# Prompt delta rule: the turns of v and k stand at other places in TensorE's order

## The reference

```python
qkv, new_conv = causal_conv(jnp.concatenate([q_a, k_a, v_a], axis=-1), conv_buf, conv_w)
qkv = jax.nn.silu(qkv.astype(f32))
q, k, v = jnp.split(qkv, [GDN_QK_WIDTH, 2 * GDN_QK_WIDTH], axis=-1)
q, k = l2norm(q) * GDN_DK ** -0.5, l2norm(k)
...
A = jnp.where(strict, jnp.einsum('nbhid,nbhjd->nbhij', kb, k) * decay, 0.0)
L = A + jnp.eye(C, dtype=A.dtype)
sol = lax.linalg.triangular_solve(L, rhs, left_side=True, lower=True, unit_diagonal=True)
u, w = sol[..., :DV], sol[..., DV:]
...
def chunk_step(S, inp):
    v_new = u_n - jnp.einsum('bhck,bhkv->bhcv', w_n, S)
    o_n = jnp.einsum('bhck,bhkv->bhcv', q_n, S) + jnp.einsum('bhij,bhjv->bhiv', qk_n, v_new)
    S = S * ge[..., None, None] + jnp.einsum('bhck,bhcv->bhkv', k_n, v_new)
```

## Time and profile before

| | |
|---|---|
| median of 3 runs | 3023.04 us (3020.31 to 3026.46) |
| profiled execution | 3019.03 us, span 3017.4 us |
| TensorE busy | 2488.4 us, 82% of the span |
| VectorE busy | 1534.6 us, 51% |
| ScalarE busy | 1060.1 us, 35% |
| GpSimd busy | 390.5 us, 13% |
| heads of the prompt delta rule begin at | 151.64, 267.12, 370.85, 473.41, 576.20, 678.75, 781.43, 883.97 us |

### The profile page before, as it was taken

One profiled execution on the slowest core, in us unless ns is written; L12 is line 12 of the kernel. 1 busy time (PEld: TensorE's weight loads), 2 busy tenths in 40 slices (PEclk: granted clock), 3 DMA queues, 4 the chain that ended last, 5 costly groups with the idle time before them and its releaser, 6 DMA issues. The chain is left out here.

```text
span 3017.4 us, 34539 instructions
## 1 busy us (share of the span) xinstructions
PE 2488.4 (82%) x12055; PEld 1842.5 (61%) x12056; DVE 1534.6 (51%) x2016; ACT 1060.1 (35%) x1517; POOL 390.5 (13%) x434
## 2 busy tenths in 40 slices
PE   4789999999995756789986989888937999999940
PEld 2367666776674633644445989883426888888720
DVE  2155455545544312124446464633346888888805
ACT  3123323322331100023333333321206777777702
POOL 1012012101201120012222000000022111111003
PEclk7899999999997757589997999999968999999965
DMA  7411111111101023031105544444246999999625
GB/s 287 169 38 37 37 30 52 36 37 30 52 5 49 19 83 129 1 84 42 42 1 195 148 125 145 127 141 151 78 176 261 401 405 406 405 403 403 258 104 188
DMA packets 313391, 436.14 MB, mean 145 GB/s; under 512 B 56354, under 2 KB 254514, under 8 KB 293539
## 3 DMA queue, kind: packets, MB, share of 16 engines
q1 hardware_dynamic: 289164, 370.93, 34.9%
q0 software_dynamic: 11168, 39.12, 3.5%
q10 hardware_dynamic: 13000, 25.30, 2.2%
HBM read 384.40 MB, written 52.94 MB: 145 GB/s over the span
## 5 line engine op out<-in xcount | busy, mean ns | idle before, releaser
L2417 DVE TENSOR_TENSOR ex_w_r<-ex_w,ex_wh 128x2048 fp32r<-128x2048 f32 x192 | 433.2, 2284 | 59.7 <-ACT ex_wh L2359 59.6
L2359 ACT ACTIVATE ex_wh<-ex_w 128x2048 fp32r<-128x2048 f32 x192 | 367.7, 1917 | 130.6 <-PEq L2066 43.0
L828 PE MATMUL gd_ps<-hT,gd_w 128*128 128x352 f32 x768 | 252.3, 483 | 8.1 <-DMA gd_w<-in_w_in_dram 7.4
L1779 PE MATMUL mg_psum<-mg_xl,mg_wh 128*128 128x352 f32 x768 | 251.4, 327 | 0.0
L828 PEld LDWEIGHTS gd_ps<-hT,gd_w 128*128 128x128 f32 x768 | 151.6, 202 | 91.0 <-issue 13.8
L1839 DVE TENSOR_TENSOR mg_w_r<-mg_w,mg_wh 128x1024 fp32r<-128x1024 f32 x96 | 133.9, 1399 | 118.8 <-ACT mg_wh L1792 118.4
L1792 ACT ACTIVATE mg_wh<-mg_w 128x1024 fp32r<-128x1024 f32 x96 | 101.3, 1056 | 183.2 <-DVE mg_out L1866 120.1
L1951 PE MATMUL op_mix<-op_w,op_mT 128*128 128x512 f32 x288 | 130.6, 613 | 25.0 <-DMA op_w<-in_w_out_dram 25.0
L1779 PEld LDWEIGHTS mg_psum<-mg_xl,mg_wh 128*128 128x128 f32 x768 | 147.7, 192 | 0.0
L1779 PE MATMUL mg_psum<-hT_r,mg_wh 128*128 128x352 f32 x384 | 126.2, 329 | 18.4 <-DVE mg_w_r L1839 18.4
L1475 PE MATMUL wp_proj_psum<-hT,wp_wq 128*128 128x512 f32 x256 | 116.2, 608 | 14.0 <-DMA wp_wk<-in_w_in_dram 8.8
(11 more groups left out here) (576 smaller groups left out, 5195.0 us busy)
## 6 DMA issues: line engine op xcount, KB each, us to landing
ex_w<-in_w_gate_dram SPq DMA_DIRECT2D x64, 1024.0 KB, 8.0
ex_w<-in_w_up_dram SPq DMA_DIRECT2D x64, 1024.0 KB, 7.4
ex_w<-in_w_down_dram SPq DMA_DIRECT2D x64, 1024.0 KB, 8.6
ada_w<-in_w_ada_dram SPq DMA_DIRECT2D x24, 1024.0 KB, 16.0
mg_w<-in_w_in_dram SPq DMA_DIRECT2D x48, 512.0 KB, 3.5
gd_w<-in_w_in_dram SPq DMA_DIRECT2D x32, 512.0 KB, 4.2
expert_out_scratch<-ex_y ACTq DMA_DIRECT2D x32, 512.0 KB, 7.7
mg_w<-in_w_br_gdn_dram SPq DMA_DIRECT2D x24, 512.0 KB, 3.9
```

The lines of the kernel that those rows point to most:

```text
L828: last = nc.tensor.matmul(dst, w[t][:, n, :], c.hT[:, n, at], start=(n == 0), stop=(n == KD - 1))
L1779: last = nc.tensor.matmul(pm[b][q][:, 0:R], a, x, start=(m == 0 and v == 0), stop=(m == KD - 1 and v == 2))
L2359: nc.scalar.activation(wh[at][:], wl[b][u][:], ACT.Copy).then_inc(w_high, 1)
L2417: nc.vector.tensor_tensor(wl_r[b][u][:], wl[b][u][:], wh[at][:].bitcast(F32), ALU.subtract).then_inc(w_low, 1)
```

## The change

Only the order of TensorE's and ScalarE's programs changes, inside `delta_prompt`. TensorE: the first unit of q of the next head comes ahead of the turn of k; the remaining units of q and the first unit of k follow it without the turn of v between them; the turn of v stands inside level four, behind both first quads and ahead of the two products with T1. In the last head there are no projections, and the turn of k keeps its place. ScalarE: the copy of q's first unit comes ahead of the copies of k, and the copies of v come behind T1 of level four. Instructions, tiles and waits are otherwise the same.

```diff
@@ ScalarE
                     evac(2, 1, i)
                     evac(2, 2, i)
+                    if nxt:
+                        evac(0, 0, i + 1)
                     for g in range(2):
                         act.wait_ge(turned, i * 2 + g + 1)
                         nc.scalar.activation(kt[g][:], X[g][0][:], ACT.Copy).then_inc(kts, 1)
-                    if nxt:
-                        evac(0, 0, i + 1)
...
                         evac(0, 1, i + 1)
                         evac(0, 2, i + 1)
-                    for g in range(2):
-                        act.wait_ge(vturned, i * 2 + g + 1)
-                        nc.scalar.activation(vt[g][:], pp[g][:], ACT.Copy, scale=0.5).then_inc(vts, 1)
                     if nxt:
                         evac(1, 0, i + 1)
                     for l in (4, 5, 6):
...
-                        if nxt and l > 4:
+                        if l == 4:
+                            for g in range(2):
+                                act.wait_ge(vturned, i * 2 + g + 1)
+                                nc.scalar.activation(vt[g][:], pp[g][:], ACT.Copy, scale=0.5).then_inc(vts, 1)
+                        elif nxt:
                             evac(1, l - 4, i + 1)
@@ TensorE
                         last.then_inc(scored, 1)
+                    if nxt:
+                        pe.wait_ge(v_evac, i * 3 + 3)
+                        for half in range(2):
+                            project(0, 0, half, i + 1)
                     for g in range(2):
                         pe.wait_ge(ats, i * 8 + g * 4 + 4)
                         turn(X[g][0], y[1], g).then_inc(turned, 1)
                     if nxt:
-                        pe.wait_ge(v_evac, i * 3 + 3)
-                        for u in range(3):
+                        for m in range(1, 4):
                             for half in range(2):
-                                project(0, u, half, i + 1)
-                    pe.wait_ge(v_silu, i + 1)
-                    pe.wait_ge(capped, i * 8 + 8)
-                    for g in range(2):
-                        turn(pp[g], y[2], g).then_inc(vturned, 1)
-                    if nxt:
-                        for half in range(2):
-                            project(1, 0, half, i + 1)
+                                project(m // 3, m % 3, half, i + 1)
                     for l in (4, 5, 6):
...
-                        if nxt and l > 4:
+                        if l == 4:
+                            pe.wait_ge(v_silu, i + 1)
+                            pe.wait_ge(capped, i * 8 + 8)
+                            for g in range(2):
+                                turn(pp[g], y[2], g).then_inc(vturned, 1)
+                        elif nxt:
                             project(1, l - 4, 0, i + 1)
                         for g in range(2):
                             pe.wait_ge(t1, i * 6 + (l - 4) * 2 + g + 1)
```

## The result

The changed kernel takes 3046.44 us (median of 5 runs, 3039.84 to 3051.42); before 3023.04 (5 runs, 3020.31 to 3031.41). The ratio is 1.0070, 95% interval 1.0053 to 1.0086: slower by 0.7%. It was measured once more beside the experiments: 3040.03 (6 runs, 3034.94 to 3046.17), ratio 1.0049, 1.0033 to 1.0065. The forecast was 3035.7, range 3027 to 3043. It was slower, as forecast, but the first measurement lies above the range; the second lies inside it.

The account below looks back on a forecast made before the run. VectorE and transfers up to the YT landing, then 72 us of TensorE, bound each head. 7 x (0.89 for v + 1.0 for the clock) + 0.9 last head - 1.4 lateness = 12.7 us on 3023.04: 3035.7, range 3027 to 3043.

Parts of the forecast that it names:

- What sets level four: Level four's second quad waits for the last YT landing, about 0.23 us behind it, not for TensorE's order.
- The moves: Ahead of level four: filled waits gain nothing, one 8 us idle, project(1, 0) waits 0.6 us, k's delay is covered.
- v's price: Between level four's second quad and next product: v's eight transposes come onto the path, 0.89 us a head at full clock.
- The lateness that goes: At level four's second quad: TensorE's lateness, 1.1 us in head 1 and 0.1 in three heads, disappears: 1.4 us off.
- The clock's term: Level four after the idle: half clock for 4.29 us from resumption, losing 1.0 us in each of heads 0 to 6.
- three rows: Slow spells before the change, after waits in heads 0, 1 and the last: 2.75, 5.84 and 4.29 us.
- Rival C: Level four: clock stays low longer, perhaps 5.84 us in every head; 18.3 us, 3041.3, or 3045 with k slipping; chance 0.11.
- The range's top: Upper end of the forecast range, 3043: the longer slow clock's 3041.3 with part of a slipped k product.
- slipped product of k: On GpSimd: a k product passing its 1.1 us to spare into the solve, about 0.5 us a head more.

Follow-up runs that it names:

- TensorE kept busy: Changed kernel with 12 matmuls of 352 columns, result unused, added behind project(1, 0) in heads 0 to 6: 3033.86 us, ratio 1.0032.

## Why the prediction was wrong

*What sets level four* was right: the second quad is 0.22 to 0.31 us behind the landing in the first seven heads, and a chain shortened by 3.7 us shortened the heads. *The moves* were right: one idle of 7.3 to 7.8 us for the 8 forecast, project(1, 0)'s wait of 0.62 for 0.6, GpSimd's first product of k right behind its mask product, no gain from the filled waits. *v's price* was right: 0.87 us a head for 0.89. *The lateness that goes* was right: 1.2 us for 1.4.

*The clock's term* was mis-sized, and this is the step that failed. The prediction took 4.29 us of slow clock from the resumption, the mean of three rows, and 1.0 us of loss in each of heads 0 to 6. The spells were 6.0 us in the mean. With the clock up, level five stands 4.0 us behind the landing (TensorE kept busy); in the changed kernel 5.7 in the mean of these heads: 1.7 us, not 1.0. The last head was put down at 0.9 for v because its quads were slow already; its spell grew from 4.29 to 6.83 us and it lost 2.0. Put together: 7 x (0.87 + 1.7) + 2.0 - 1.2 = 18.8 us, which is the 18.8 of the two profiles; the forecast's sum was 12.7. Rival C's first number, 18.3, was the nearer, with the 5.84 us of head 1 for every head. Its reason, the wait between the two quads, is not shown, so that it came so near is in part luck. The three rows ran from 2.75 to 5.84 us, and one mean was made to stand for all heads. Why the spells came out longer than these rows stays open; the runs show that the pause is not needed for a long spell and does not always make one, and that the spell is what is left of the slow stretch when TensorE resumes, a stretch that was 10.24 us in most heads and not in all.

The rule cited of the Trainium skill (TensorE: Matmul & The Clock Gate, "HAM oscillation — how this bites in real kernels") held: a burst behind a wait for a transfer began at half clock in all eight heads, behind waits of 7.3 us and more.

*The range's top* was C's 3041.3 with part of a slipped product of k. The slip did not come, and nothing was added there for the spread of the runs: the kernel before itself spreads over 3013 to 3038, and the two medians of the changed kernel, 3046 and 3040, lie 6 apart.

## What to carry to other kernels

An idle engine is not the path: before filling a wait, follow the other chain that reaches the next join, and ask where the idle will stand afterwards. Work taken out of a wait that a transfer covers was free there; behind the landing v cost its full 0.87 us a head, and the idle that the moves had gathered ahead of level four (7.3 to 7.8 us) left the clock at half over it, another 1.7. To gain, move work from behind the landing into the idle (27 us here), shorten the chain that sets the landing, or both (53 us).

## What the runs showed of the hardware

- The slow spell behind an idle is no constant. Counted from TensorE's resumption at level four it was 3.4 to 6.9 us in the two profiles of the changed kernel (means 6.0 and 5.5). Without any break after the resumption it was 2.9 to 3.8 in the eight heads of one kernel, and 2.8 to 3.3 in four heads and 5.2 to 5.3 in four of another.
- Matmuls whose result is thrown away made a kernel faster: 24 passes a head, 168 in all, shortened the stretch of the eight heads from 834.0 and 832.0 us to 821.6 in the profiles; the ratio is 1.0032, against 1.0070 and 1.0049.
- With the solve moved ahead, its first three steps on VectorE took 0.77 to 0.98 us each while GpSimd's products ran, and the next one 0.18. In the kernel before one step alone, beside the last of these products, took as long (0.80), and the following ones 0.18. By these durations, of one head each, some 1.6 us of what the earlier solve could win went there (an estimate).
